# First layer: the scan's input coefficient formed beside the first norms, the keys' power and scaling taken earlier

## The chip, the cores and the metric

The kernel runs on one core of one Trainium2 chip. The metric is the device time of one execution in microseconds (us). Before the change three runs gave 987.22, 986.7 and 988.71 us, the median being 987.22 us.

## The reference

Two transformer blocks run one after the other on a sequence of 256 tokens and a width of 1024, in 32-bit floats. The first block has two layers. Each layer normalises, projects, and mixes the tokens in three ways: an S5 state space model on 256 channels, a gated spatial product on 256, and differential attention on 512. A convolution-gated MLP follows. The second block has dilated window, grouped and memory attention, with a gated merge. The change touches only the first layer of the first block, and there these two parts:

```python
# S5 mixer
lam = a_re + 1j * a_im
a_bar = exp(lam * dt)
b_bar = ((a_bar - 1.0) / lam)[..., None] * b_mat      # the input coefficient
bu = einsum("bsgh,gph->bsgp", u, b_bar)
states = associative_scan(a_bar, bu)
y = real(einsum("bsgp,ghp->bsgh", states, c_mat))

# differential attention
q = apply_rope(rms_norm(q, q_gain)); k = apply_rope(rms_norm(k, k_gain))
s = einsum(q, k) * scale                              # then a softmax by heads
```

The input coefficient is (a_bar - 1) / lam, one complex number for each group and state, held as 128 partitions by 16 columns. The kernel folds it into the output matrix c. The keys are scaled by the inverse root of their mean square, a power that GpSimd computes.

## The kernel before

**Weights.** Every product of activations with weights is made of three fp32r products: high part by high part, high by low, low by high. The weights stream through in 294 pairs of 128x1024. SyncE loads a pair into one of seven buffers `raw` (L432). ScalarE rounds it to its high part `whi` (L1100, six buffers). VectorE subtracts for the low part `wlo` (L1710, seven buffers). TensorE multiplies (L557 to L559 tile by tile for the queries, L594 to L596, L601 to L603) and counts the pairs it has used; ScalarE may overwrite a `whi` only once the pair six before is used. Pairs 0 to 3 are the queries, 4 to 7 the keys, 8 and 9 the channels of the state space model, 10 to 13 those of the spatial product, 14 to 17 the values.

**Order.** The order of the work is written out by hand, engine by engine. On VectorE `lo_upto(n)` stands wherever the low parts up to pair n are to be made, and the work of norms, attention and scan stands between these calls. `link` puts an instruction on a chain semaphore and, unless told otherwise, makes the next instruction wait for it.

**VectorE, first layer.** It prepares the state space parameters (L1744 to L1756), scales token tile 0 (L1719, `norm_scale`), and corrects its transposes (L1728, `norm_lo(0, 0)`). Then it takes the first amplitude power (L1764 to L1767), scales tile 1, prepares the phases (L1773 to L1778), and corrects tile 1 (`norm_lo(0, 1)`, again L1728). TensorE can multiply tile 1 only after that. The rotary tables follow (L1821), then for queries and keys a sum of squares by head (L1842), two products with the tables (L1830, L1831) and the rotation (L1835, L1836). Between queries and keys stands `coefficients()`, 15 linked instructions (L1788 to L1802). After the keys' rotation stand `phase_turns` (L353 to L355), pair 12, and the scaling of the keys (L1922). Then `rotate` turns the scan's inputs (L1847, L1848, L1853, L1854). It waits for the input products of TensorE and for the tables `etab`, which ScalarE makes from the turns (L364 to L369). After it come pair 14, the maxima of the first scores (L1864, L1867), `lambdas()`, pairs 15 and 16, and the two scans (L1939).

**GpSimd, first layer.** It powers the sums of squares (L1544 to L1546), builds the powers of the amplitude (L1569 to L1572), and expands the input matrix for its two parts c = 0 and 1 (`input_powers`: L411, L412, L414, L415). Then follow the queries' power (L1580, L1581), small work (L1596 to L1603), the fold of the coefficient into the output matrix (`folded`: L1551, L384 to L386), the keys' power (L1533, L1534), and the output powers, six instructions of 128x1024 (L396, L398, L400, twice). The fold waits for VectorE's coefficient, the keys' power for the keys' sum of squares.

**TensorE, first layer.** Query tile 0, transposes, query tile 1, key pairs 4 to 7 with transposes between, pairs 8 and 9, input products (L702), pairs 10 and 11, transposes of the keys (L757), pairs 12 and 13, first scores (L774), pairs 14 and 15, Toeplitz products (L676), pair 16, and so on. ScalarE rounds pair 16 (L1100) and then makes `etab`.

## Time and profile before

| | |
|---|---|
| median of three runs | 987.22 us |
| lowest, highest run | 986.7, 988.71 us |
| profiled execution, span | 986.2 us |
| TensorE busy | 954.6 us, 97% |
| VectorE busy | 695.7 us, 71% |
| ScalarE busy | 546.8 us, 55% |
| GpSimd busy | 258.5 us, 26% |

The profiled execution's own time is known here by its span, 986.2 us, alone; the lowest run lies 0.5 us above it and the median 1.0 us, which is what lies around the span. An engine's busy share says how much of the span it worked, not whether it set the end. For that the chain of waits is followed: it goes back from the last instruction, at each step to what released it. A timeline row gives start, duration, engine, line, operation, shapes, how many instructions are merged in it, and in brackets how long the engine sat idle before and what ended that.

### The profile page before, as it was taken

How to read it: one execution, taken by the hardware profiler on the slowest of the kernel's cores; microseconds unless marked ns; L12 is line 12 of the kernel's file. 1: busy time of each engine (PE TensorE's matmuls, PEld its weight loads, DVE VectorE, ACT ScalarE, POOL GpSimd, SP SyncE). 2: the span in 40 equal slices, each digit the busy share in tenths (PEclk: the TensorE clock that was granted, in tenths of full speed). 3: DMA queues.
4: the chain of work that ended last, by engine and by line, in shares of the span. 5: the costliest groups of instructions: out<-in, count | busy, mean ns of one | idle time of the engine just before them, and what ended most of it. 6: DMA issues, size and time to landing. Idle time of an engine off the chain costs nothing.

```text
span 986.2 us, 15775 instructions
## 1 busy us (share of the span) xinstructions
PE 954.6 (97%) x6139; PEld 838.7 (85%) x6143; DVE 695.7 (71%) x1074; ACT 546.8 (55%) x900; POOL 258.5 (26%) x196
## 2 busy tenths in 40 slices
PE   6979999999999999999999999999999999999997
PEld 4867789999978887799999988899787889888886
DVE  6998658778865688586777765558576755666785
ACT  7746556656743746756665554453454554555633
POOL 4890101676800021200455500003121300000030
PEclk9999999999999999999999999999999999999999
DMA  7622356665655542456665666575544445654452
GB/s 283 231 85 86 108 177 188 191 191 174 186 181 169 167 151 86 158 163 198 182 188 192 183 193 194 178 212 173 169 152 148 134 151 172 197 168 149 149 188 84
DMA packets 48473, 165.95 MB, mean 168 GB/s; under 512 B 6544, under 2 KB 7056, under 8 KB 48400
## 3 DMA queue, kind: packets, MB, share of 16 engines
q1 hardware_dynamic: 48400, 164.95, 53.2%
q8 instruction: 49, 0.80, 0.3%
q14 instruction: 24, 0.20, 0.1%
HBM read 162.83 MB, written 1.05 MB: 166 GB/s over the span
## 4 chain that ended last, share of the span: by engine, by line
PE 83%; DVE 9%; ACT 4%; issue 2%; POOL 1%; DMA 0%; DVEq 0%; POOLq 0%; SPq 0%; ACTq 0%
PE PJ L601 13%; PE PJ L603 13%; PE PJ L602 13%; PE PJ L596 10%; PE PJ L594 10%; PE PJ L595 10%; DVE wlo L1710 2%; PE PJ L557 2%; PE PJ L559 2%; PE PJ L558 2%; PE T L1041 1%; ACT whi L1100 1%; PE T L1032 1%; PE PJ L744 1%; PE S L648 1%
## 5 line engine op out<-in xcount | busy, mean ns | idle before, releaser
L1710 DVE TENSOR_TENSOR wlo<-raw,whi 128x1024 fp32r<-128x1024 f32 x294 | 370.3, 1290 | 95.8 <-ACT whi L1100 93.4
L1100 ACT ACTIVATE whi<-raw 128x1024 fp32r<-128x1024 f32 x294 | 303.0, 1062 | 77.1 <-DMA raw<-weights_in 70.5
L594 PE MATMUL PJ<-xthb,whi 128*128 128x256 f32 x864 | 242.9, 281 | 0.9 <-DVE wlo L1710 0.5
L596 PE MATMUL PJ<-xthb,wlo 128*128 128x256 f32 x864 | 242.3, 280 | 0.0
L595 PE MATMUL PJ<-xtlb,whi 128*128 128x256 f32 x864 | 241.4, 279 | 0.0
L601 PE MATMUL PJ<-whi,xthb 128*128 128x512 f32 (+1 forms) x432 | 173.9, 403 | 5.1 <-DVE wlo L1710 5.1
L603 PE MATMUL PJ<-whi,xtlb 128*128 128x512 f32 (+1 forms) x432 | 167.2, 387 | 0.0
L602 PE MATMUL PJ<-wlo,xthb 128*128 128x512 f32 (+1 forms) x432 | 167.0, 387 | 0.0
L594 PEld LDWEIGHTS PJ<-xthb,whi 128*128 128x128 f32 x864 | 163.0, 189 | 1.5 <-issue 1.3
L595 PEld LDWEIGHTS PJ<-xtlb,whi 128*128 128x128 f32 x864 | 163.0, 189 | 0.2
L596 PEld LDWEIGHTS PJ<-xthb,wlo 128*128 128x128 f32 x864 | 162.9, 189 | 0.0
L1632 POOL TENSOR_TENSOR gtd<-acc 128x512 f32<-128x512 f32 x22 | 96.4, 4380 | 149.2 <-ACT acc L1347 140.9
L2068 DVE SCALAR_TENSOR_TENSOR acc<-PJ,colv,acc 128x255 f32<-128x255 f32 (+1 forms) x176 | 72.5, 475 | 55.5 <-ACT acc L1342 54.8
L601 PEld LDWEIGHTS PJ<-whi,xthb 128*128 128x128 f32 x432 | 81.3, 188 | 25.6 <-issue 9.0
L1342 ACT ACTIVATE acc<-PJ,colv 128x256 f32<-128x256 f32 x88 | 42.5, 564 | 96.5 <-PE PJ L596 96.5
L603 PEld LDWEIGHTS PJ<-whi,xtlb 128*128 128x128 f32 x432 | 81.1, 188 | 17.2
L602 PEld LDWEIGHTS PJ<-wlo,xthb 128*128 128x128 f32 x432 | 81.4, 188 | 14.5
L601 PE MATMUL PJ<-whi,hth 128*128 128x512 f32 x144 | 56.1, 390 | 0.9 <-DVE wlo L1710 0.9
L603 PE MATMUL PJ<-whi,htl 128*128 128x512 f32 x144 | 56.0, 389 | 0.0
L602 PE MATMUL PJ<-wlo,hth 128*128 128x512 f32 x144 | 56.0, 389 | 0.0
L1689 POOL TENSOR_TENSOR merged<-merged,gt 128x512 f32<-128x512 f32 x6 | 9.6, 1625 | 160.7 <-DVE gt L2292 160.7
L601 PEld LDWEIGHTS PJ<-whi,hth 128*128 128x128 f32 x144 | 27.0, 188 | 6.8 <-issue 1.3
(399 smaller groups left out, 1341.1 us busy)
## 6 DMA issues: line engine op xcount, KB each, us to landing
raw<-weights_in SPq DMA_DIRECT2D x294, 512.0 KB, 3.6
rt<-bmerge_in SPq DMA_DIRECT2D x6, 256.0 KB, 4.2
xres<-x_in SPq DMA_DIRECT2D x2, 512.0 KB, 5.6
memx<-mem_in SPq DMA_DIRECT2D x2, 512.0 KB, 4.1
y_out<-xn SPq DMA_DIRECT2D x4, 256.0 KB, 2.3
rowv<-rows_in SPq DMA_DIRECT2D x1, 576.0 KB, 10.6
ptmp<-bexp_in SPq DMA_DIRECT2D x2, 256.0 KB, 6.6
cex<-cexp_in SPq DMA_DIRECT2D x2, 256.0 KB, 8.6
```

The lines of the kernel that those rows point to most:

```text
L557: pe.matmul(o, h, wh, start=(j == 0 and kk == 0), stop=False, skip_group_check=True)
L594: pe.matmul(o, a, xh[:, k, :], start=(first and f % 2 == 0), stop=False, skip_group_check=True)
L595: pe.matmul(o, a, xl[:, k, :], start=False, stop=False, skip_group_check=True)
L596: m = pe.matmul(o, b, xh[:, k, :], start=False, stop=last, skip_group_check=True)
L601: pe.matmul(o, h, wh, start=first, stop=False, skip_group_check=True)
L602: pe.matmul(o, h, wl, start=False, stop=False, skip_group_check=True)
L603: m = pe.matmul(o, lw, wh, start=False, stop=last, skip_group_check=True)
L1100: act.activation(whi[:, p % HIGHS, :], raw[:, p % LOADS, :], ACT.Copy).then_inc(hi_ready, 1)
L1342: act.activation(acc[:, j % 2, i, :], PJ[BUF[c]][:, i // 2, (i % 2) * TOK:(i % 2 + 1) * TOK], ACT.Identity, scale=colv[:, k + 2:k + 3], bi ...
L1632: pool.tensor_tensor(gtd[:, j % 2, :, :], acc[:, j % 2, 0:2, :], acc[:, j % 2, 2:4, :], ALU.mult).then_inc(sem("gated"), 1)
L1710: dve.tensor_tensor(wlo[:, p % LOADS, :], raw[:, p % LOADS, :], whi[:, p % HIGHS, :].bitcast(F32), ALU.subtract).then_inc(lo_ready, 1)
L2068: dve.scalar_tensor_tensor(out=acc[:, j % 2, i, sh:TOK], in0=PJ[BUF[c]][:, i // 2, (i % 2) * TOK:(i % 2 + 1) * TOK - sh], scalar=colv[:, k ...
```

## The change

Four things are moved, all in the first layer.

- The input coefficient is formed in other places and with 13 instructions instead of 15. Seven (new lines L1760 to L1766) stand before the scaling of tile 0, and give are/(are²+aim²) and aim/(are²+aim²). Six (L1788 to L1793), of 16 or 32 columns, stand after the phase preparation and before `norm_lo(0, 1)`. `coefficients()` is gone. In the fold rows 11 and 12 of the parameters change places.
- GpSimd takes the keys' power before the fold instead of after it.
- VectorE scales the keys before pair 12 and `phase_turns`, instead of after both.
- VectorE makes pairs 15 and 16 before `lambdas()` instead of after it.

```diff
@@ -376,7 +376,7 @@
         def fold_coefficient(eng, link, l, tmp):
 
             eng.wait_ge(sem("cex_landed"), 16 * (l + 1))
-            cr, ci, nci, ncr = (wide(sp_[:, r, 8 * l:8 * l + 8], 32, 2) for r in (9, 10, 11, 12))
+            cr, ci, nci, ncr = (wide(sp_[:, r, 8 * l:8 * l + 8], 32, 2) for r in (9, 10, 12, 11))
             re, im = cex[:, 0, :, :], cex[:, 1, :, :]
             t = tmp[:, 0:256].rearrange("p (s h) -> p s h", s=ST)
             for c, (i0, k0, i1, k1) in enumerate(((re, cr, im, nci), (re, nci, im, ncr))):
@@ -1601,8 +1601,8 @@
             link(pool.tensor_tensor(skip[:, 0:64], ident[:, 0:64], ident[:, 64:128], ALU.add))
             link(pool.tensor_tensor(skip[:, 0:32], skip[:, 0:32], skip[:, 32:64], ALU.add))
             link(pool.tensor_copy(ident4.rearrange("p (t h) -> p t h", t=STEP), wide(skip[:, 0:32], STEP)))
+            head_powers(0, 1)
             folded(0)
-            head_powers(0, 1)
             output_powers(pool, link, 0, 0, ptmp)
             output_powers(pool, link, 0, 1, ptmp)
             pool.sem_inc(sem("gpow_ready"), 1)
@@ -1756,6 +1756,14 @@
             link(dve.tensor_scalar(v[5], v[5], 3.1415925, -3.1415925, ALU.min, ALU.max))
 
             dve.sem_inc(sem("par_ready"), 1)
+            are, aim = col("are"), col("aim")
+            link(dve.tensor_tensor(v[16], are, are, ALU.mult), False)
+            link(dve.tensor_tensor(v[17], aim, aim, ALU.mult))
+            link(dve.tensor_tensor(v[16], v[16], v[17], ALU.add))
+            link(dve.reciprocal(v[13], v[16]))
+            link(dve.tensor_tensor(v[16], are, v[13], ALU.mult), False)
+            link(dve.tensor_tensor(v[15], aim, v[13], ALU.mult), False)
+            link(dve.tensor_tensor(v[17], aim, v[13], ALU.mult))
             norm_scale(0, xres, 0)
             lo_upto(1)
             norm_lo(0, 0)
@@ -1766,7 +1774,6 @@
             link(dve.tensor_tensor(apw[:, 0, 1, :], v[3], v[8], ALU.mult), False)
             link(dve.tensor_tensor(apw[:, 1, 1, :], v[3], v[6], ALU.mult))
             dve.sem_inc(sem("par_ready"), 1)
-            v[15] = apw[:, 1, 1, :]
             lo_upto(3)
             norm_scale(0, xres, 1)
             lo_upto(4)
@@ -1776,31 +1783,20 @@
             link(dve.tensor_tensor(v[19], v[19], v[18], ALU.subtract))
             link(dve.memset(chunks[:, :], 1.0))
             link(dve.tensor_tensor_scan(chunks[:, :], chunks[:, :], chunks[:, :], -1.0, ALU.mult, ALU.add))
+
+            from_one = apw[:, :, :, :].rearrange("p c t n -> p (c t) n")[:, 0:STEP + 3:STEP + 2, :]
+            link(dve.tensor_scalar(apw[:, 0, 0, :], apw[:, 0, 1, :], -1.0, None, ALU.add))
+            link(dve.tensor_tensor(sp_[:, 22:24, :], from_one, sp_[:, 16:18, :], ALU.mult), False)
+            link(dve.tensor_tensor(sp_[:, 13:15, :], from_one, sp_[:, 15:17, :], ALU.mult))
+            link(dve.tensor_tensor(v[9], v[22], v[23], ALU.add), False)
+            link(dve.tensor_tensor(v[10], v[14], v[13], ALU.subtract))
+            link(dve.tensor_scalar(sp_[:, 11:13, :], sp_[:, 9:11, :], -1.0, None, ALU.mult))
+            dve.sem_inc(sem("par_ready"), 1)
             norm_lo(0, 1)
             lo_upto(7)
             dve.wait_ge(sem("cst_landed"), 32)
             cosv = cs("cos").rearrange("p (t d) -> p t d", t=TT)
             sinv = cs("sin").rearrange("p (t d) -> p t d", t=TT)
-
-            def coefficients():
-
-                are, aim = col("are"), col("aim")
-                link(dve.tensor_scalar(v[14], apw[:, 0, 1, :], -1.0, None, ALU.add))
-                link(dve.tensor_tensor(v[16], are, are, ALU.mult))
-                link(dve.tensor_tensor(v[17], aim, aim, ALU.mult))
-                link(dve.tensor_tensor(v[16], v[16], v[17], ALU.add))
-                link(dve.reciprocal(v[16], v[16]))
-                link(dve.tensor_tensor(v[17], v[14], are, ALU.mult))
-                link(dve.tensor_tensor(v[18], v[15], aim, ALU.mult))
-                link(dve.tensor_tensor(v[17], v[17], v[18], ALU.add))
-                link(dve.tensor_tensor(v[9], v[17], v[16], ALU.mult))
-                link(dve.tensor_tensor(v[17], v[15], are, ALU.mult))
-                link(dve.tensor_tensor(v[18], v[14], aim, ALU.mult))
-                link(dve.tensor_tensor(v[17], v[17], v[18], ALU.subtract))
-                link(dve.tensor_tensor(v[10], v[17], v[16], ALU.mult))
-                link(dve.tensor_scalar(v[11], v[10], -1.0, None, ALU.mult))
-                link(dve.tensor_scalar(v[12], v[9], -1.0, None, ALU.mult))
-                dve.sem_inc(sem("par_ready"), 1)
 
             def lambdas():
 
@@ -1904,9 +1900,6 @@
                 head_sums(0)
                 lo_upto(s0 + 8)
                 rotary(0, A, "q_terms", "q_rot", s0 + (10 if l else 9))
-                if l == 0:
-                    lo_upto(s0 + 10)
-                    coefficients()
                 lo_upto(s0 + 11)
                 if l:
                     dve.wait_ge(sem("mixw_landed"), 32 * (l + 1))
@@ -1914,14 +1907,13 @@
                     lo_upto(s0 + 13)
                 head_sums(1)
                 rotary(1, B, "k_terms", "k_rot", s0 + (14 if l else 12))
-                if l == 0:
-                    phase_turns(dve, link, 0)
-                    lo_upto(s0 + 13)
                 dve.wait_ge(sem("hr_ready"), 2 * l + 2)
                 k8 = heads8(xn[:, :, 512:1024])
                 dve.tensor_tensor(k8, k8, wide(hr[:, 1, :].rearrange("p (t g) -> p t g", t=TT), QKD, 3), ALU.mult)\
                    .then_inc(sem("k_scaled"), 1)
                 if l == 0:
+                    lo_upto(s0 + 13)
+                    phase_turns(dve, link, 0)
                     dve.wait_ge(sem("mixw_landed"), 32)
                     dve.memset(wsts[64:128, :, 0:64], 0.0).then_inc(sem("wst_ready"), 1)
                 lo_upto(s0 + (17 if l else 14))
@@ -1967,8 +1959,8 @@
                 else:
                     lo_upto(s0 + 15)
                     batch_max(0)
+                    lo_upto(s0 + 17)
                     lambdas()
-                    lo_upto(s0 + 17)
                     scans()
                     lo_upto(s0 + 18)
                     gate_rows()
```

VectorE between tile 1's scaling and the rotary tables. Before:

```order
L1776 TENSOR_TENSOR sp_<-sp_ 128x16
L1777 MEMSET chunks 128x64
L1778 SCALAR_TENSOR_TENSOR chunks<-chunks 128x64
L1728 SCALAR_TENSOR_TENSOR xtlb<-T,colv,xthb 128x128 x8
L1710 TENSOR_TENSOR wlo<-raw,whi 128x1024 x3
```

Now:

```order
L1783 TENSOR_TENSOR sp_<-sp_ 128x16
L1784 MEMSET chunks 128x64
L1785 SCALAR_TENSOR_TENSOR chunks<-chunks 128x64
L1788 TENSOR_SCALAR apw<-apw 128x16
L1789 TENSOR_TENSOR sp_<-apw,sp_ 128x32
L1790 TENSOR_TENSOR sp_<-apw,sp_ 128x32
L1791 TENSOR_TENSOR sp_<-sp_ 128x16
L1792 TENSOR_TENSOR sp_<-sp_ 128x16
L1793 TENSOR_SCALAR sp_<-sp_ 128x32
L1728 SCALAR_TENSOR_TENSOR xtlb<-T,colv,xthb 128x128 x8
L1710 TENSOR_TENSOR wlo<-raw,whi 128x1024 x3
```

Six instructions now stand ahead of the eight corrections of tile 1, on which TensorE's second query tile waits.

VectorE from the keys' rotation to the scan's rotation. Before:

```order
L1836 TENSOR_TENSOR xn<-qh,sm 128x2x8x32
L353 TENSOR_TENSOR md<-sp_,chunks 128x512
L354 TENSOR_SCALAR md<-md 128x512
L355 SCALAR_TENSOR_TENSOR md<-md 128x512
L1710 TENSOR_TENSOR wlo<-raw,whi 128x1024
L1922 TENSOR_TENSOR xn<-xn,hr 128x2x512
L1926 MEMSET wsts 64x4x64
L1710 TENSOR_TENSOR wlo<-raw,whi 128x1024
L1847 TENSOR_TENSOR qh<-T,etab 128x1024
```

Now:

```order
L1832 TENSOR_TENSOR xn<-qh,sm 128x2x8x32
L1912 TENSOR_TENSOR xn<-xn,hr 128x2x512
L1710 TENSOR_TENSOR wlo<-raw,whi 128x1024
L353 TENSOR_TENSOR md<-sp_,chunks 128x512
L354 TENSOR_SCALAR md<-md 128x512
L355 SCALAR_TENSOR_TENSOR md<-md 128x512
L1918 MEMSET wsts 64x4x64
L1710 TENSOR_TENSOR wlo<-raw,whi 128x1024
L1843 TENSOR_TENSOR qh<-T,etab 128x1024
```

The scaling of the keys is now first of this group; the turns, from which ScalarE makes `etab`, have two instructions fewer between them and the rotation.

GpSimd, from the small work to the output powers, as a difference:

```order
 L1603 COPY cst<-cst 128x128
+L1533 TENSOR_SCALAR hr<-hsk 128x16
+L1534 TENSOR_TENSOR hr<-hr,mhalf 128x16
 L1551 TENSOR_SCALAR cst<-cst,colv 128x128 x2
 L384 TENSOR_TENSOR gpw<-cex,sp_ 128x8x32
@@ -46,6 +48,4 @@
 L385 TENSOR_TENSOR ptmp<-cex,sp_ 128x256
 L386 TENSOR_TENSOR gpw<-gpw,ptmp 128x8x32
-L1533 TENSOR_SCALAR hr<-hsk 128x16
-L1534 TENSOR_TENSOR hr<-hr,mhalf 128x16
 L396 TENSOR_TENSOR gpw<-gpw,apw 128x8x128
```

The keys' power has moved ahead of the eight instructions of the fold, which now wait behind it.

## Rows read from the trace of the kernel before

**Rows 1.** Page, part 1 (engine, busy us and share, instructions) and part 4 (chain that ended last).

```profile
PE 954.6 (97%) x6139; PEld 838.7 (85%) x6143; DVE 695.7 (71%) x1074; ACT 546.8 (55%) x900; POOL 258.5 (26%) x196
...
PE 83%; DVE 9%; ACT 4%; issue 2%; POOL 1%; DMA 0%; DVEq 0%; POOLq 0%; SPq 0%; ACTq 0%
```

**Rows 2.** Timeline of DVE, 7 to 23 us (start, duration, engine, line, operation, idle before).

```profile
7.76 0.88 DVE L1719 TENSOR_SCALAR xn<-xres,rstd 128x512 f32<-128x512 f32 x2 [2.76 <-POOL rstd L1546]
...
19.17 0.29 DVE L1778 TENSOR_TENSOR_SCAN chunks<-chunks 128x64 f32<-128x64 f32 x1
...
20.91 2.16 DVE L1728 SCALAR_TENSOR_TENSOR xtlb<-T,colv,xthb 128x128 fp32r<-128x128 f32 x8 [1.44 <-ACT xthb L1120]
```

**Rows 3.** Timeline of POOL, 19 to 27 us.

```profile
19.57 0.40 POOL L411 COPY vm<-bex 128x256 f32<-128x256 f32 x1
...
19.93 1.52 POOL L412 TENSOR_TENSOR vm<-bex,apw 128x768 f32<-128x768 f32 x1
...
21.41 1.53 POOL L414 TENSOR_TENSOR ptmp<-bex,apw 128x768 f32<-128x768 f32 x1
...
23.02 4.02 POOL L415 TENSOR_TENSOR vm<-vm,ptmp 128x768 f32<-128x768 f32 x1
```

**Rows 4.** Chain of waits, 28 to 34 us (start, duration, engine, tile, line), and POOL's timeline.

```profile
28.56 1.52 DVE ropeq L1821
...
28.35 1.57 POOL L412 TENSOR_TENSOR kmT<-bex,apw 128x768 f32<-128x768 f32 x1
...
31.53 1.86 POOL L415 TENSOR_TENSOR kmT<-kmT,ptmp 128x768 f32<-128x768 f32 x1
```

**Rows 5.** Stretches: PE busy, PEld, DVE, ACT, POOL (x instructions), PEclk, DMA.

```profile
21.57:45.58 24.01, 24.01 (x137) 21.03 (x138) 22.65 (x36) 18.27 (x26) 20.34 (x17) 1.00 0.64 215
```

**Rows 6.** Timeline of DVE, 42 to 46 us.

```profile
42.03 0.29 DVE L1788 TENSOR_SCALAR sp_<-apw 128x16 f32<-128x16 f32 x1
...
45.31 0.17 DVE L1802 TENSOR_SCALAR sp_<-sp_ 128x16 f32<-128x16 f32 x1
```

**Rows 7.** Timeline of ACT, 55 to 59 us.

```profile
55.02 1.06 ACT L1100 ACTIVATE whi<-raw 128x1024 fp32r<-128x1024 f32 x1 [5.78 <-PE PJ L603]
...
57.81 0.63 ACT L369 ACTIVATE etab<-md 128x512 f32<-128x512 f32 x1
```

**Rows 8.** Timeline of DVE, 54 to 73 us.

```profile
56.06 3.00 DVE L1922 TENSOR_TENSOR xn<-xn,hr 128x1024 f32<-128x1024 f32 x1
...
61.90 1.21 DVE L1847 TENSOR_TENSOR qh<-T,etab 128x1024 f32<-128x1024 f32 x1
...
64.28 0.69 DVE L1853 TENSOR_TENSOR sw<-qh 128x512 f32<-128x512 f32 x1
...
64.89 2.46 DVE L1854 TENSOR_TENSOR sw<-qh 128x512 f32<-128x512 f32 x1
...
67.27 2.98 DVE L1710 TENSOR_TENSOR wlo<-raw,whi 128x1024 fp32r<-128x1024 f32 x1
...
71.61 0.92 DVE L1867 SCALAR_TENSOR_TENSOR st_<-st_,hr 128x8 f32<-128x8 f32 x1
```

**Rows 9.** Timeline of POOL, 64 to 73 us.

```profile
64.34 2.46 POOL L396 TENSOR_TENSOR gpw<-gpw,apw 128x1024 f32<-128x1024 f32 x1
...
69.25 3.25 POOL L400 TENSOR_TENSOR gpw<-gpw,ptmp 128x1024 f32<-128x1024 f32 x1
```

**Rows 10.** Timeline of PE, 59 to 76 us.

```profile
59.12 1.09 PE L757 MATMUL S<-cst,xn 128*128 128x128 f32 x8 [1.49 <-DVE xn L1922]
...
70.39 0.47 PE L601 MATMUL PJ<-whi,xthb 128*128 128x512 f32 x1 [3.15 <-DVE wlo L1710]
```

**Rows 11.** Stretch at 400 us, columns as in Rows 5, then PE's timeline.

```profile
400.00:402.00 2.00, 1.93 (x5) 1.60 (x6) 0.00 (x0) 1.67 (x5) 0.00 (x0) 0.50 0.90 367
...
400.07 3.57 PE L744 MATMUL PJ<-md,wglus 128*128 128x256 f32 x8 [0.94 <-issue]
...
101.18 1.97 PE L744 MATMUL PJ<-md,wglus 128*128 128x256 f32 x8 [0.94 <-issue]
```

## The prediction

> **What bounds the kernel now.** I read the page first, then the chain of waits, then the timelines of the engines over the first 105 us. TensorE is busy for 97% of the span and makes up 83% of the chain; VectorE has 9% [rows 1]. Behind the first layer's attention TensorE hardly waits, so a change here pays only if it lets TensorE begin that run sooner. Before it, through most of the first layer, the chain runs through VectorE. TensorE waits there 1.49 us for the scaled keys and 3.15 us for the low part of pair 14 [rows 10].
>
> Two stretches matter. In the first, TensorE works from 21.57 to 45.58 us with no gap: 24.01 busy of 24.01 us [rows 5]. It begins when VectorE has corrected the first transposes of tile 1, which VectorE starts at 20.91 us after 1.44 us idle [rows 2]. In the second, VectorE rotates the scan's inputs at 61.90 us [rows 8]. ScalarE had the tables for it at 57.81 + 0.63 = 58.44 us. These tables stand behind ScalarE's rounding of pair 16, which began at 55.02 us, the moment TensorE had used pair 10 [rows 7].
>
> **The part that is removed.** `coefficients()` runs from 42.03 to 45.31 + 0.17 = 45.48 us [rows 6]. With the issue of the next pair that is 3.6 us on VectorE's path. The next pairs' high parts are there by then, so VectorE really moves up. But it can't use all of it. The tables of ScalarE hang on TensorE's pair 10 and not on VectorE, so the rotation can't start before 58.44 us. The cap is 61.90 - 58.44 = 3.46 us.
>
> **The seven early instructions.** VectorE sits idle for 2.76 us before it scales tile 0 [rows 2]. Small linked instructions follow each other every 0.21 us (15 took 3.45 us, with their waits [rows 6]), so seven take at most 1.5 us. They are done before GpSimd delivers the first norm. Cost: nothing. If that cover were gone, they would cost those 1.5 us on the first transposes.
>
> **The six later instructions.** They start when the scan of the chunks ends, at 19.17 + 0.29 = 19.46 us. Alone they would take six times 0.21 us or less, 1.25 us, and end by 20.7 us, before 20.91 us. But GpSimd expands the input matrix at that time: L411 from 19.57, L412 from 19.93, L414 from 21.41, L415 from 23.02 us [rows 3]. What that does to a small VectorE instruction with two operands in SBUF is seen later. The rotary table of 128x128 that starts at 28.56 us takes 1.52 us and ends at 30.08; GpSimd's L412 runs from 28.35 to 29.92 us [rows 4]. L1867, 128x8, takes 0.92 us and ends at 72.53 us, when L400 ends at 72.50 [rows 8, 9]. So a VectorE instruction, however small, waits until a GpSimd instruction under way is over, and gets in before the next. The six are four links: L1788; L1789 with L1790; L1791 with L1792; L1793. The first gets through before L411 reads. The second meets L411, and L1790 or the third meets L412, to 19.93 + 1.52 = 21.45 us. The link behind that meets L414, to 21.41 + 1.53 = 22.94 us. The rest, two issues, gets in before L415 reads. The corrections then start at about 23.2 us in place of 20.91, and **TensorE's tile 1 is 2.3 us late**. Bounds: nothing if no instruction is held; if the last one is also held by L415, which takes 1.86 us where it is free [rows 4], the start is 23.10 + 1.86 = 24.96 us and the loss 4.05. I take 2.3 since two of the three holds follow whatever the order at the first one.
>
> The Trainium skill (SBUF — State Buffer, Who interferes with whom) says that VectorE with two SBUF inputs and GpSimd exclude each other for a whole instruction, and that the one issued first keeps the port. By that, rows 4, 8 and 9 agree, and the six instructions are held; without it they would be free and the change would give the whole 3.46 us.
>
> **The sum.** TensorE carries these 2.3 us without loss to pair 10, since it has no gap to absorb them [rows 5]. So ScalarE's tables come at 58.44 + 2.3 = 60.74 us, and the rotation starts at 60.74 in place of 61.90: 1.16 us sooner. VectorE waits there for them, with nothing left of its own lead.
>
> **Keys.** L1922 ended at 59.06 us, held by GpSimd for 1.8 of its 3.00 us (L1847, of as many columns, takes 1.21) [rows 8]. Now the power no longer stands behind the fold, and the scaling not behind the turns and a pair; VectorE reaches it 3.6 us (coefficients) and some 3 us (turns and a pair) before 56.06 us, so near 49.5 us, and near 52 us with TensorE's delay. TensorE's wait of 1.49 us before L757 goes [rows 10], and 2.3 come in, so its first scores end 0.8 us later, near 68.1 us. The wait for pair 14 up to 70.39 us covers this [rows 10]. What is late next is pair 14 itself, on VectorE. GpSimd's fold, moved behind the power, costs it an idle start but the products that read its output powers stand behind pairs 14 and 15 on TensorE, of 12 matmuls each, at least 5 us after 70.39 us, and the powers ended at 72.50 [rows 9, 10].
>
> **Lambdas.** Pairs 15 and 16 come some 1.4 us sooner, but VectorE's next scan does not, since the same instructions stand before it, and from there the chain goes on through VectorE. Cost and gain: nothing on the path; TensorE's wait before pair 15 only moves to a later place. If VectorE were no longer on the path, this part would be worth up to 1.4 us.
>
> **The phase of the holds.** From the rotation on VectorE's L1853, L1854 and pair 14 alternate with GpSimd's output powers. Before, the second and third were held: 2.46 and 2.98 us, against 0.69 for L1853 [rows 8]. With both engines shifted, there may be one hold more or one less, 1.8 us each way. TensorE's first scores set the other end: 70.25 (end of pair 14) - 68.1 = 2.2 us gain at most. So this case gives a gain between -0.7 and 2.2, and I take 1.2.
>
> 987.22 - 1.2 = **986.0 us**, own range 985.0 to 987.9. In the profiled execution the span of 986.2 would become 985.0; the median of the runs lies 1.0 us above the span.
>
> **Rivals.**
> 1. *The six instructions slip through.* They are 16 or 32 columns wide, and the trace shows no such instruction at the back-to-back boundary of L411 and L412. Against it stands L1867, as narrow and held [rows 8, 9]. Then all 3.46 us come: 983.8 us, with the phase of the holds 982.0 to 985.6.
> 2. *Slower: one hold more, and TensorE's clock.* L1793 is held by L415. Tile 1 starts 4.05 us late, TensorE is idle for over 4 us, and the rotation starts 4.05 - 3.46 = 0.6 us later than before: 987.8 us. The point from which it decides is 3.46 us of delay. If in addition the granted clock falls to 0.50, which is 1.2 of 2.4 GHz, as it did at 400 us after two pauses (L744 took 3.57 us there, 1.97 in the first layer [rows 11]), TensorE loses 1.6 us more, before pair 10: 3.46 - 4.05 - 1.6 = -2.2, so 989.4 us. For it: the pause is longer than any behind which the clock stayed up (3.15 us [rows 10]).
> 3. *The holds eat it.* GpSimd's fold starts after the keys' power and later than before relative to VectorE, so the output powers meet VectorE at one more place: 1.2 - 1.8, and 987.2 us once L1867's own hold of 0.75 us (0.92 less the 0.17 of so narrow an instruction as L1802) is free. The change does then what it says, and nothing comes of it.
>
> The Trainium skill (TensorE: Matmul & The Clock Gate, What's actually happening) says that an idle TensorE is put back to half its clock. Here 400 us agrees, and the pause before 70.39 us does not. By the page rival 2 would deserve more than I give it.
>
> **How the numbers follow.** Forecast 0.45; rival 1 0.25; rival 2 0.15 (0.07 at 987.8, 0.08 at 989.4); rival 3 0.15. A measurement of this kernel tells about 0.2% from no change, 2.0 us, so faster means below 985.2 and slower above 989.2. Faster: nearly all of rival 1 (0.23) and the far edge of the forecast (0.07), 0.30. Slower: 0.08 of rival 2 and a little for a clock fall at another place, where every pause now lies at another time (1.6 us each), 0.10. The rest, 0.60, is the same. The range reaches from 983.6, the likeliest of rival 1, to 988.6, and leaves out the fall of the clock and the far edge of rival 1.
>
> **What would show it.** In the new profile: six small instructions at 19.5 us that end near 20.7 (rival 1), 23.2 (forecast) or 25 us (rival 2), one or two of them 1.4 us long; the start of tile 1 on TensorE at 21.6, 23.9 or 25.6 us; the rotation's start at ScalarE's tables and no longer behind a pair; no TensorE wait before L757; how often L1853, L1854 and pair 14 are over 1.3 us long; the granted clock at 20 to 30 us and at 400 us. I would be wrong in the step itself if the rotation still started behind VectorE's own work, or if TensorE had caught up its delay before pair 10.

## The result, and the profile after

The change makes the kernel slower. Six runs have a median of 991.43 us (990.97 to 993.49), and six of the kernel before, taken with them, 987.41 us (986.7 to 988.71): a ratio of 1.0034, 95% interval 1.0024 to 1.0044. The forecast was 986.0 us with 983.6 to 988.6 as its range, and 0.10 for slower. (The ratio, here and in the table below, is the estimate on record and not the quotient of the two medians, which is 1.0041 here: the loss is 3.4 us by the one and 4.0 by the other.) The profiled execution is the slowest of the six, 993.49 us, with a span of 991.7 us, 5.5 more than before, so its rows show more of the loss than the median has.

The page, part 1 and the chain's shares, which answer to [rows 1]. VectorE has less of the chain (9% before, 7% now), but TensorE has more of it (83% before, 86% now):

```profile
PE 959.7 (97%) x6139; PEld 842.9 (85%) x6143; DVE 689.4 (70%) x1072; ACT 547.2 (55%) x900; POOL 262.5 (26%) x196
...
PE 86%; DVE 7%; ACT 4%; issue 2%; POOL 1%; DMA 0%; DVEq 0%; POOLq 0%; SPq 0%; ACTq 0%
```

**First place, 19 to 34 us.** The timeline of VectorE (start, duration, line, idle before), then of TensorE:

```profile
19.66 0.17 DVE L1788 TENSOR_SCALAR apw<-apw 128x16 f32<-128x16 f32 x1
19.86 0.31 DVE L1789 TENSOR_TENSOR sp_<-apw,sp_ 128x32 f32<-128x32 f32 x1
20.10 0.18 DVE L1790 TENSOR_TENSOR sp_<-apw,sp_ 128x32 f32<-128x32 f32 x1
20.31 1.38 DVE L1791 TENSOR_TENSOR sp_<-sp_ 128x16 f32<-128x16 f32 x1
21.62 0.16 DVE L1792 TENSOR_TENSOR sp_<-sp_ 128x16 f32<-128x16 f32 x1
21.81 1.39 DVE L1793 TENSOR_SCALAR sp_<-sp_ 128x32 f32<-128x32 f32 x1
23.35 2.16 DVE L1728 SCALAR_TENSOR_TENSOR xtlb<-T,colv,xthb 128x128 fp32r<-128x128 f32 x8
...
24.01 0.79 PE L557 MATMUL PJ<-whi,xthb 128*128 128x512 f32 x1 [3.08 <-DVE xtlb L1728]
```

Two of the six instructions last 1.38 and 1.39 us instead of 0.17, each until one of GpSimd's is over (at 21.66 and 23.16 us):

```profile
20.09 1.57 POOL L412 TENSOR_TENSOR vm<-bex,apw 128x768 f32<-128x768 f32 x1
21.62 1.54 POOL L414 TENSOR_TENSOR ptmp<-bex,apw 128x768 f32<-128x768 f32 x1
```

The corrections start at 23.35 us (20.91 before [rows 2]), TensorE at 24.01 (21.57 before [rows 5]). Then comes what the forecast's sum had not counted. Stretches of TensorE (bounds, length, busy us of PE, PEld, DVE, ACT, POOL with their instructions, then PEclk, DMA share, GB/s):

```profile
22.00:26.00 4.00, 1.99 (x5) 1.60 (x6) 3.85 (x10) 2.42 (x5) 3.76 (x4) 0.64 0.01 2
26.00:30.00 4.00, 4.00 (x11) 3.13 (x10) 4.00 (x3) 1.06 (x1) 4.00 (x2) 0.50 0.34 126
30.00:34.00 4.00, 4.00 (x19) 3.28 (x19) 3.93 (x4) 1.94 (x2) 3.25 (x2) 1.00 0.83 270
```

The granted clock fell to 0.50, which is 1.2 of 2.4 GHz, in the pause of 3.08 us, and was up again by 30 us: 11 matmuls in 4 us at the one level, 19 at the other. The 24 matmuls of tile 1 took 8.5 us instead of 5.7.

**Second place, 60 to 80 us.** ScalarE's rounding of pair 16 and the last of its tables, then VectorE:

```profile
60.25 1.06 ACT L1100 ACTIVATE whi<-raw 128x1024 fp32r<-128x1024 f32 x1 [5.80 <-PE PJ L603]
...
63.05 0.63 ACT L369 ACTIVATE etab<-md 128x512 f32<-128x512 f32 x1
```

```profile
63.88 1.23 DVE L1843 TENSOR_TENSOR qh<-T,etab 128x1024 f32<-128x1024 f32 x1 [4.07 <-ACT etab L369]
...
66.27 2.43 DVE L1849 TENSOR_TENSOR sw<-qh 128x512 f32<-128x512 f32 x1
68.62 2.45 DVE L1850 TENSOR_TENSOR sw<-qh 128x512 f32<-128x512 f32 x1
70.99 2.98 DVE L1710 TENSOR_TENSOR wlo<-raw,whi 128x1024 fp32r<-128x1024 f32 x1
...
75.33 0.89 DVE L1863 SCALAR_TENSOR_TENSOR st_<-st_,hr 128x8 f32<-128x8 f32 x1
...
79.78 2.48 DVE L1931 TENSOR_TENSOR_SCAN sw<-decay,sw 128x512 f32<-128x512 f32 x2
```

Pair 16 is rounded 5.23 us later than before [rows 7]: 2.4 by the held instructions, and 2.8 on the way from there, which e2 below puts down to the clock. The rotation starts at the tables, as forecast, 1.98 us later than before instead of 1.16 sooner. Then L1849 is held too (2.43 us, 0.69 before [rows 8]), which makes 3.69 us at the scans, 79.78 where the trace before has 76.09:

```profile
76.09 2.48 DVE L1939 TENSOR_TENSOR_SCAN sw<-decay,sw 128x512 f32<-128x512 f32 x2
```

GpSimd's timeline tells why there is one hold more:

```profile
52.03 4.02 POOL L1551 TENSOR_SCALAR cst<-cst,colv 128x128 f32<-128x128 f32 x2
...
61.76 1.99 POOL L396 TENSOR_TENSOR gpw<-gpw,apw 128x1024 f32<-128x1024 f32 x1
...
72.96 3.23 POOL L400 TENSOR_TENSOR gpw<-gpw,ptmp 128x1024 f32<-128x1024 f32 x1
```

Its six output powers run from 61.76 to 76.19 us, from 55.25 to 72.50 before. The fold in front of them starts at 52.03 us, in VectorE's run of two-input instructions, and its first two take 4.02 us; they took 1.35 us before.

**Third place, 104 us.** TensorE's gate products, which answer to [rows 11]:

```profile
104.87 3.58 PE L744 MATMUL PJ<-md,wglus 128*128 128x256 f32 x8 [0.94 <-issue]
```

They took 1.97 us before behind the same pause of 0.94 us; now the clock is at 0.51 from 105 to 108 us. From here on the distance is 5.4 us (405.50 against 400.07 us for the same products of the second layer) and 5.5 at the end.

Between the second and the third place this trace has one more fall, which the kernel before does not have in its own: 0.59 from 74 to 76 us and 0.56 from 76 to 78, behind a pause of 3.36 us ahead of pair 14.

```profile
74.11 0.57 PE L601 MATMUL PJ<-whi,xthb 128*128 128x512 f32 x1 [3.36 <-DVE wlo L1710]
```

It cost the path nothing that the rows show: the distance is 3.69 us at the scans and still 3.69 at the start of the gate's products (104.87 against 101.18).

### The profile page after: what moved, and what is told of

It reads as the page before. It is cut to its first block, busy times and chain, and to the rows that moved or that the text cites. A ratio compares the mean times of both kernels' runs of the same rounds, so it can differ in the third digit from the quotient of the medians.

```text
span 991.7 us, 15774 instructions
## 1 busy us (share of the span) xinstructions
PE 959.7 (97%) x6139; PEld 842.9 (85%) x6143; DVE 689.4 (70%) x1072; ACT 547.2 (55%) x900; POOL 262.5 (26%) x196
## 4 chain that ended last, share of the span: by engine, by line
PE 86%; DVE 7%; ACT 4%; issue 2%; POOL 1%; DMA 0%; DVEq 0%; POOLq 0%; SPq 0%; ACTq 0%
PE PJ L601 14%; PE PJ L603 13%; PE PJ L602 13%; PE PJ L596 10%; PE PJ L594 10%; PE PJ L595 10%; PE PJ L557 2%; PE PJ L558 2%; PE PJ L559 2%; DVE wlo L1710 2%; PE T L1041 1%; ACT whi L1100 1%; PE T L702 1%; PE PJ L744 1%; PE T L1032 1%
## 5 line engine op out<-in xcount | busy, mean ns | idle before, releaser
L1710 DVE TENSOR_TENSOR wlo<-raw,whi 128x1024 fp32r<-128x1024 f32 x294 | 365.9, 1276 | 95.4 <-ACT whi L1100 93.4
```

Of the source, the lines that this page charges most:

```text
L1710: dve.tensor_tensor(wlo[:, p % LOADS, :], raw[:, p % LOADS, :], whi[:, p % HIGHS, :].bitcast(F32), ALU.subtract).then_inc(lo_ready, 1)
```

## The experiments

Two theories went in. **H**: the held coefficient instructions, and the clock behind them. **O**: GpSimd's output powers, put behind a later fold, hold VectorE around the scan's rotation. All times are medians over the 4 (e5) to 12 executions of five rounds; the kernel before was run beside each group and lay between 987.68 and 988.30 us. Only one execution of each kernel has a trace. The last three columns are from that one: start of the rotation, end of the last output power, start of the scans (us).

```
kernel                         time    ratio [95%]             rot    powers  scans
before                         -       -                       61.90  72.50   76.09
change                         991.43  1.0034 [1.0024,1.0044]  63.88  76.19   79.78
e1  GpSimd waits               990.47  1.0020 [1.0011,1.0028]  62.71  73.33   76.92
e2  TensorE kept busy          989.84  1.0015 [1.0005,1.0025]  61.47  73.82   77.41
e3  six at the old place       989.87  1.0012 [1.0002,1.0022]  58.33  75.24   76.49
e4  coefficient alone          990.33  1.0013 [1.0003,1.0022]  65.70  71.80   78.59
e5  e1, fold first             997.10  1.0099 [1.0084,1.0114]  72.48  71.48   84.64
e6  e3, fold first             995.67  1.0078 [1.0066,1.0091]  70.54  69.53   82.09
e7  keys alone                 991.86  1.0042 [1.0030,1.0054]  60.01  75.31   78.36
e8  e5, lambdas first          994.68  1.0077 [1.0064,1.0089]  72.11  71.10   83.69
e9  e3, diagonals first        988.07  0.9996 [0.9987,1.0006]  59.96  72.38   75.97
e10 e1, diagonals first        987.80  1.0003 [0.9993,1.0013]  59.67  72.43   76.03
e11 e3, three powers out       985.51  0.9973 [0.9961,0.9984]  58.50  66.20   72.38
e12 before, three powers out   985.93  0.9972 [0.9963,0.9982]  61.85  64.20   72.42
e13 e9, two fillers            992.25  1.0045 [1.0028,1.0061]  59.89  72.35   75.95
e14 before, two fillers        991.56  1.0037 [1.0023,1.0050]  61.78  72.38   75.98
e15 e2, two fillers            993.61  1.0057 [1.0041,1.0072]  60.97  73.32   76.91
e16 e9, filler at pair 14      989.49  1.0015 [1.0005,1.0025]  59.71  72.17   75.75
e17 before, filler at pair 14  987.87  0.9999 [0.9990,1.0009]  62.03  72.63   76.23
e18 e2, filler at pair 14      990.66  1.0029 [1.0018,1.0041]  64.05  72.34   78.52
```

### The change undone in parts: e1 to e4

**e1** lets GpSimd expand the input matrix only when the coefficient is there:

```diff
             pool.wait_ge(sem("bex_ready"), 1)
+            pool.wait_ge(sem("par_ready"), 4)
             input_powers(pool, link, 0, 0, x_tile(0), ptmp)
```

> The change, but GpSimd begins to expand the input matrix only when VectorE has finished the six later coefficient instructions. Theory H (holds, then clock): the six instructions lost 2.4 us to GpSimd's L412 and L414, the pause of TensorE that came of it let the granted clock fall, and both together made pair 10 5.2 us late. Here nothing holds them: the corrections of tile 1 start near 21.0 us instead of 23.35, TensorE has no pause over 1 us there and no clock of 0.50 before 70 us, the scan's rotation starts near 58.7 us, and the time is 983.0 to 985.5 us, below before. Rival O (order): what lost the time is the new order of power, fold and scaling, whose output powers meet VectorE at another place; then the time stays near the change's, 989 to 992 us, though the corrections come early.

The six now run free, 0.17 to 0.19 us each. VectorE's timeline:

```profile
20.35 0.18 DVE L1794 TENSOR_SCALAR sp_<-sp_ 128x32 f32<-128x32 f32 x1
20.77 2.16 DVE L1729 SCALAR_TENSOR_TENSOR xtlb<-T,colv,xthb 128x128 fp32r<-128x128 f32 x8 [0.24 <-ACT xthb L1120]
```

Yet the kernel is no faster than before, and H by itself falls. The test is not a clean one, though (e3 is): in its trace TensorE's clock fell at another place, with no pause but the 0.71 us ahead of L702 (0.70 in the kernel before, behind which the clock stayed up): the stretch 54 to 56 us has PE busy for 2.00 of 2.00 us at 0.50, where the kernel before has 1.00.

```profile
54.00:56.00 2.00, 2.00 (x6) 1.61 (x6) 1.82 (x4) 0.00 (x0) 1.84 (x3) 0.50 0.00 0
```

**e2** leaves the holds and keeps TensorE busy in the pause ahead of tile 1 (26 transposes of the identity into the bank that is written next):

```diff
+                if l == 0:
+                    keep_busy(B[:, 1, :], 26)
                 tile_pairs(f"q{l}", 1, 0, range(4), xth, xtl, ready=32 * l)
```

> The change, with 26 transposes of the identity into a free bank between TensorE's tile 0 and tile 1 of the queries, so that it is not idle while the corrections are late. Theory H: the corrections still start near 23.35 us and tile 1 near 24.0 us, but the granted clock stays at 1.00, the 24 matmuls of tile 1 take 5.5 us instead of 8.5, pair 10 is 2.4 us late instead of 5.2, and the time is 2.5 to 3.5 us under the change's: 987.5 to 989. Rival O: no difference to the change beyond 1 us, since the order stays.

L1728 starts at 23.72 us, as late as in the change, but the clock stays up. From the corrections to the rounding of pair 16 it takes 34.1 us instead of 36.9:

```profile
24.00:26.00 2.00, 2.00 (x13) 1.71 (x12) 2.00 (x9) 1.25 (x4) 1.83 (x3) 1.00 0.02 4
```

So the fall behind the 3.08 us pause cost 2.8 us on this path. Scans at 77.41 us, 1.32 later than before; the time is above what H gave and still above before. By the ratios the fillers take away 1.9 of the change's 3.4 us and leave 1.5.

**e3** puts the six back between the queries' and the keys' rotation (after pair 10), where the old 15 stood:

```diff
                 rotary(0, A, "q_terms", "q_rot", s0 + (10 if l else 9))
+                if l == 0:
+                    lo_upto(s0 + 10)
+                    coefficients()
```

> The change, with the seven early instructions where the change has them, but the six later ones put back at the old place of the coefficients, between queries and keys. Theory H: they cost 1.1 us on VectorE there in place of 3.6, the corrections start near 20.9 us, the clock stays up, the rotation starts at ScalarE's tables near 58.6 us, and the time is 983.0 to 985.5 us. Rival O: 989 to 992 us.

Here the whole lead is there: the rotation starts at 58.33 us, 3.57 sooner than before. And the scans start 0.40 us *later*. VectorE's timeline shows where it went, two pairs and a 128x4 instruction:

```profile
68.90 4.13 DVE L1710 TENSOR_TENSOR wlo<-raw,whi 128x1024 fp32r<-128x1024 f32 x2
72.95 2.31 DVE L1806 TENSOR_SCALAR hb<-colv 128x4 f32<-128x4 f32 x1
```

They took 2.36 and 0.16 us in the kernel before. L1806 ends when GpSimd's last power does:

```profile
72.03 3.21 POOL L400 TENSOR_TENSOR gpw<-gpw,ptmp 128x1024 f32<-128x1024 f32 x1
```

**e4** makes only the coefficient's change (order of GpSimd, keys and lambdas as in the kernel before).

> The kernel before with the coefficient's change alone: GpSimd's power after the fold, the keys scaled after the turns, lambdas first. Theory H: slower than before by about as much as the whole change, 989.5 to 992.5 us, with the corrections at 23.3 us and a clock of 0.50 behind it. Rival O: faster than before by up to 3 us, 984.5 to 987.

The time lies inside H's range, but at 1.3 us by its ratio the loss is less than half of the whole change's 3.4, and H had said about as much. The six are held as in the change (corrections at 23.18 us), the clock is at 0.51 from 24 to 26 us, and it falls again at 54.7. The tables come at 65.50 us, so the last output power, though it ends at 71.80 us and 0.70 sooner than before, meets the rotation's last product (L1850, 2.86 us), and the scans start 6.79 us behind it where it was 3.59.

### The order of the fold and the keys: e5 to e8

**e5** is e1, and **e6** is e3, with GpSimd's fold ahead of the keys' power again:

```diff
-            head_powers(0, 1)
             folded(0)
+            head_powers(0, 1)
```

> The change, with GpSimd waiting for the coefficient before it expands the input matrix (as in e1), and with the fold taken before the keys' power again, as in the kernel before. Theory of two causes (H: the held coefficient instructions and the fall of TensorE's clock behind them; O: the fold behind the keys' power makes GpSimd's output powers late, and these hold VectorE around the scan's rotation): with both away the lead of VectorE comes through as far as ScalarE's tables let it. Corrections of tile 1 at 20.8 us, tables near 58.5, rotation near 58.7, output powers from 51 to 54 us on, the maxima's last instruction at 69 to 71 us (72.53 before), the scans at 73 to 74.5 (76.09). Time 983.5 to 986 us against some 987.5 of the kernel before. H alone: already reached in e1, so no better than e1, 990. O alone: the same as the two causes. Rival (clock): TensorE's granted clock falls somewhere else once its pauses lie elsewhere, 1.6 us for each 3.4 us at 0.50, and takes the lead back: maxima and scans early as above, but 986.5 to 989 us.

> The change with the six later coefficient instructions at the coefficient's old place (as in e3), and the fold before the keys' power again. Seven instructions stay early, so VectorE is some 2.4 us ahead of the kernel before there. Theory of two causes: corrections of tile 1 at 19.7 to 20.9 us, rotation near 58.3 us, output powers from 52 to 55 us, and no such holds of pairs 14 to 16 as in e3 (4.13 us for two, and 2.31 for the lambdas' first instruction); scans at 73 to 75 us where e3 had 76.49; 983.5 to 986.5 us. If e3's scans were late for another reason (the order of pairs 15, 16 and the lambdas), they stay at 76 to 77 us and the time at 987 to 990.

They lie 11.1 and 9.2 us above the upper ends of their forecasts, the worst misses of the study. VectorE in e5:

```profile
56.16 2.94 DVE L1913 TENSOR_TENSOR xn<-xn,hr 128x1024 f32<-128x1024 f32 x1 [4.71 <-POOL hr L1534]
59.02 2.98 DVE L1711 TENSOR_TENSOR wlo<-raw,whi 128x1024 fp32r<-128x1024 f32 x1
61.93 2.88 DVE L353 TENSOR_TENSOR md<-sp_,chunks 128x512 f32<-128x512 f32 x1
64.84 2.07 DVE L354 TENSOR_SCALAR md<-md 128x512 f32<-128x512 f32 x1
66.94 2.33 DVE L355 SCALAR_TENSOR_TENSOR md<-md 128x512 f32<-128x512 f32 x1
```

VectorE waits 4.71 us for the power, behind which GpSimd begins the output powers at once. So the scaling, pair 12 and the three turns come each behind one of them, the turns take 7.3 us together (0.69 + 0.43 + 0.69 us in the kernel before), and the tables come at 71.77 us. O as stated (early powers are good) falls; what is left of it is that the *number of VectorE's instructions that meet a power* counts. With the keys scaled ahead of the turns, the power has to stand ahead of the fold; the reverse, the power moved alone, was not run.

**e7** makes these two parts alone in the kernel before:

> The kernel before with the keys' part alone: GpSimd takes the keys' power ahead of the fold, VectorE scales the keys ahead of pair 12 and the turns. The coefficient stays as it was, the lambdas too. Theory O: output powers start 2 to 4 us later than the 55.25 us of before, meet the rotation and pair 14, and the maxima's last instruction and the scans come 0.5 to 2 us later (scans 76.6 to 78): 987.5 to 990 us. H alone: this order does nothing (TensorE's wait for the scaled keys goes, pair 14 sets the end): scans at 76.1, 986.5 to 988 us. My prediction's reading of the part, a gain by the phase turns having fewer instructions behind them, would give 985.5 to 987.

It is at least as slow as the whole change (ratio 1.0042 against 1.0034). The rotation starts 1.89 us sooner, the scans 2.27 us later. Output powers from 60.93 to 75.31 us hold the second product of the rotation, pair 14 and two of the lambdas' sums, of which one row:

```profile
73.00 2.39 DVE L1813 CUSTOM_DVE_ANT_0 sqs<-ug 128x64 f32<-128x64 f32 x1
...
78.36 2.48 DVE L1938 TENSOR_TENSOR_SCAN sw<-decay,sw 128x512 f32<-128x512 f32 x2
```

TensorE then pauses 4.13 us ahead of pair 14 and 3.07 ahead of pair 15, and its clock falls in both:

```profile
69.27 0.76 PE L601 MATMUL PJ<-whi,xthb 128*128 128x512 f32 x1 [4.13 <-DVE wlo L1710]
...
77.45 0.77 PE L601 MATMUL PJ<-whi,xthb 128*128 128x512 f32 x1 [3.07 <-DVE wlo L1710]
```

**e8** is e5 with `lambdas()` ahead of pairs 15 and 16 again.

> As the first kernel of this call, and the lambdas before pairs 15 and 16 again, as in the kernel before. It tells what the move of the lambdas is worth when the lead is there. Prediction's reading: up to 1.4 us if VectorE isn't on the path and nothing if it is, so the same as the first kernel within 0.5 us, or up to 1.4 us slower. Rival: the lambdas behind two pairs meet GpSimd's last output power (in e3 their first instruction took 2.31 us), so with them first this kernel is 0.5 to 2 us faster than the first: scans below 73 us.

Its median is 2.4 us lower, on five executions against four and with intervals that overlap. The lambdas don't show in it: from the end of the maxima to the scans it is 3.56 us in e5 and 3.57 in e8, since the powers are over by then. The scans of e8 start 0.95 us sooner in its trace, all of it from ahead of that stretch; what makes up the rest was not found.

### The shared stretch: e9 to e12

A third theory: from the keys' rotation to the scans, GpSimd's fold and powers and VectorE's instructions take turns, and a lead of VectorE only meets more of them. **e9** (on e3) and **e10** (on e1) take GpSimd's first two instructions of the fold, which need no coefficient, into its idle time ahead of the keys' power:

```diff
+            skip_diagonals(0)
             head_powers(0, 1)
             folded(0)
```

> As e3 (coefficient's six at the old place, power before the fold), but GpSimd takes the two scalings of the skip diagonal (first lines of the fold, which need no coefficient) before the keys' power, where it sat idle for 3.00 us in e3. Theory of the shared stretch: from the keys' rotation to the scans the end is set by GpSimd's work that must lie there, fold and output powers, and every lead of VectorE is eaten by holds until the last output power ends (75.24 us in e3). The two scalings took 4.02 us there, so the output powers start some 3 to 4 us sooner, near 55 to 56 us instead of 58.92, end near 71 to 72.5, and the scans come at 73 to 75 us instead of 76.49. Time: 1.5 to 3.5 us less than e3, so 986.5 to 988.5 against 988 of before in the last measurement. Rival: GpSimd is starved by VectorE's run of two-input instructions (48 to 59 us) whatever it executes, and the powers still start at 58 us or later: time as e3. Clock rival: scans as forecast, but falls of the granted clock add 1.6 us each.

> As e1 (GpSimd waits for the coefficient before the input matrix) with the two scalings before the keys' power. There GpSimd was idle for only 0.83 us before the power, so the scaling delays the power by about 0.5 us, which VectorE hardly meets (keys scaled at 50.3 to 51 us). Shared stretch theory: output powers start near 55 to 56 us instead of 58.73, end near 70 to 71 instead of 73.33, scans at 74 to 75.5 instead of 76.92. If the clock stays up at 52 us, tables at 59 instead of 62.5 us and another 1 us. Time 986 to 989 us (e1: 990.47).

The last power ends 2.86 us sooner in e9 than in e3, and 0.90 in e10 than in e1. Times fall by 1.8 and 2.7 us, to that of the kernel before, and no lower: the scans stand at 75.97 and 76.03 us, with the rotation 1.9 and 2.2 us earlier than before. The scans moved by only 0.5 and 0.9 us, so part of what the times gained came from elsewhere. In e9 all of L1858, L1859, pair 14 and L1872 are held:

```profile
62.34 2.56 DVE L1858 TENSOR_TENSOR sw<-qh 128x512 f32<-128x512 f32 x1
64.81 2.44 DVE L1859 TENSOR_TENSOR sw<-qh 128x512 f32<-128x512 f32 x1
67.18 2.97 DVE L1716 TENSOR_TENSOR wlo<-raw,whi 128x1024 fp32r<-128x1024 f32 x1
```

**e11** (on e3) and **e12** (on the kernel before) put one fill with zeros in the place of the last three output powers, the imaginary half of them:

```diff
             output_powers(pool, link, 0, 0, ptmp)
-            output_powers(pool, link, 0, 1, ptmp)
+            link(pool.memset(gpw[:, 1, :, 1:STEP + 1, :], 0.0))
```

> e3 with the last three of the six output powers left out and one fill of the same tile with zeros in their place. Left out: the imaginary half of the output powers in the first layer. Shared stretch theory: the lead now gets through: the last output power ends near 65 to 66 us, pairs 15 and 16 take 1.2 us each, the lambdas' first instruction 0.2 us, scans at 72 to 73.5 us (76.49 in e3); time 984 to 986.5 us. If the powers are not what holds the scans, they stay at 75.5 us or later and the time near 989.

> The kernel before with the same three output powers left out. Shared stretch theory: the holds behind 64.3 us go (second product of the rotation 1.8, pair 14 1.8, maxima's last instruction 0.75 us; TensorE's first scores allow some 2.2 to 3 of it): scans at 73 to 74 us, 985 to 987 us. So it gains as the kernel with the lead does, and what is between the two, 0.5 to 1.5 us of the 3.5 us of lead, is what the lead is worth when the powers are out of the way. If VectorE's own length set the end, the two would differ by the whole 3.5 us.

Both kernels lie below before, by 2.8 and 2.4 us by their medians (2.7 and 2.8 by the ratios), and the scans of both at 72.4 us: first e11, then e12.

```profile
72.38 2.48 DVE L1937 TENSOR_TENSOR_SCAN sw<-decay,sw 128x512 f32<-128x512 f32 x2
```

```profile
72.42 2.47 DVE L1939 TENSOR_TENSOR_SCAN sw<-decay,sw 128x512 f32<-128x512 f32 x2
```

With three powers fewer the scans start 4.11 us sooner than in e3 and 3.67 sooner than before: the powers hold them back in both kernels. And a rotation that starts 3.35 us sooner (58.50 against 61.85) is again worth 0.04 us. But that the two agree is in part chance, since the maxima ahead of the scans (67.20 and 67.23 us) are released by different things. In e11 pair 14 is held by a power, which ends at 66.20 us because the fold started late; in e12 the powers are over at 64.20, nothing holds pair 14, and VectorE waits for TensorE's first scores. Pair 14 and GpSimd's power in e11, then the maxima in e12:

```profile
63.92 3.37 DVE L1710 TENSOR_TENSOR wlo<-raw,whi 128x1024 fp32r<-128x1024 f32 x1
63.52 2.68 POOL L400 TENSOR_TENSOR gpw<-gpw,ptmp 128x1024 f32<-128x1024 f32 x1
```

```profile
67.23 1.42 DVE L1864 TENSOR_REDUCE st_<-S 128x4 f32<-128x512 f32 x2 [0.56 <-PE S L774]
```

In e11 those scores are there at 65.37 us, 1.8 sooner than in e12 (67.18). So the lead is not worthless by itself: it was lost to the powers that are left.

The two last columns of the table now read as one sum: the scans start when the last power has ended and VectorE has done what it then has left. In every trace but e12's the last power holds an instruction of VectorE. In the kernel before, the change, e1, e2, e9, e10 and e13 to e17 it is the maxima's last one, and the scans come 3.58 to 3.60 us behind the power. In e3 and e7 it is one of the lambdas, and they come 1.25 and 3.05 us behind. In e11 and e18 it is pair 14, in e4 the rotation's last product and in e5, e6 and e8 pair 13, and they come 6.2 to 13.2 us behind. So in e3 the lead was worth 2.34 us (3.59 less 1.25), and the power that ends 2.74 us later than before takes that back and 0.40 more.

### The clock: e13 to e18

`keep_busy` transposes the identity. **e13, e14, e15** (on e9, before, e2) do it ahead of pair 14 and ahead of the gate's products:

```diff
                 if l == 0:
+                    emptied("v0")
+                    keep_busy(PJ[buf("v0")][:, 0, :], 22)
                     project("v0", pairs=[0, 1])
...
+                    if l == 0:
+                        pe.wait_ge(sem("da_exp"), 16)
+                        keep_busy(S1, 8)
                     pe.wait_ge(sem("g_ready"), 2 * (l + 1))
```

> As e9 (scans at 75.97 us, as before; median 988.07), and TensorE transposes the identity 22 times while it waits for pair 14 and 8 times before the gate's products near 100 us. Clock theory: e9's falls at 69.9 and 100.7 us go, 1.6 us each, with scans unchanged at 76.0 us: 984.5 to 986.5 us, and below the kernel before in this call. Rival: the falls only move to another pause, or the fillers lie in TensorE's way (0.12 us each): 987 to 989 us.

> The kernel before with the same fillers. Its profile shows no fall at 70 or 100 us, but its runs range over 4 us, so some of them have falls somewhere. Clock theory: 985.5 to 987.5, up to 1.5 us below before in this call, with fewer runs above 988. Rival (fillers cost or do nothing): within 0.5 us of before or slower.

> The change with 26 fillers ahead of tile 1 (as e2) and the two groups of the last two kernels. Clock theory: no falls at 23, 70 to 75 and 103 to 105 us, scans at 77.4 us as in e2, 1.3 us later than before: 986.5 to 988.5 us, so 1.3 us above the second kernel of this call, and what is left of the loss is the holds. Rival: the loss is not the clock's: 989.5 to 991.5 us, as e2 or more.

These measured their own mistake. The eight fillers wait for the last exponentials, which end at 102.0 us, so TensorE pauses for 1.97 us where it had 0.94, starts the gate's products 2.65 us later, and the clock is at 0.50 from 102 to 106 us. In e14:

```profile
102.10 1.94 PE L628 MATMUL S<-cst 128*128 128x128 f32 x8 [1.97 <-ACT sm L1247]
103.83 3.62 PE L747 MATMUL PJ<-md,wglus 128*128 128x256 f32 x8
```

**e16, e17, e18** are the same without the eight.

> e9 with the 22 fillers ahead of pair 14 only. Clock theory: the fall at 70 us goes, the one at 100 us may stay or go; scans at 76.0, TensorE's gate products at 101.1 us: 985.5 to 987.5 us, at least 1 us below before in this call if both falls go. Rival: the fall only comes elsewhere: 987.5 to 988.5 us, as e9.

> The kernel before with the 22 fillers ahead of pair 14 only. It had no fall there, so: the same as before within 0.5 us (987.5 to 988.5), scans 76.1, gate products 101.1 us. If a pause filled here lets the clock stay up at the later pauses as well, up to 1.5 us less.

> The change with 26 fillers ahead of tile 1 and 22 ahead of pair 14. Holds alone: scans 0.8 to 1.3 us later than before (76.9 to 77.4), so 0.8 to 1.3 us above the second kernel of this call, 988.5 to 989.5. If the clock still falls once more than there (at 103 us), another 1.6 us: 990 to 991. If the median of e2 (989.84) isn't undercut, the fall at 74 us was not part of the loss.

e17 is the kernel before. e16 is 1.4 us slower than e9 although the fall at 70 us is gone from its profile and the scans are as early; nothing in its profile explains that. Its executions have a mean granted clock of 0.9936 against e9's 0.9950, so falls at other places are one reading, but no trace shows them, and it stays open. e18 is 0.8 us above e2 and 0.8 below the change: its profile has the fall of the kind seen in e1 and e4, at 53 us, and by its own expectation a median that doesn't undercut e2's says that the fall at 74 us was not part of the loss. So a filler takes a fall away from one pause, and what the clock does at the next place isn't in hand.

How much of the loss is the clock? The mean granted clock over the span was 0.9927 in the six of the change and 0.9945 to 0.9959 in those of the kernel before (11 to 35 in each group). The difference, 0.0018 to 0.0032, of 988 us would be 1.8 to 3.2 us of TensorE's time at full clock. That is an estimate from above: not every fall lies on the path (the one at 74 us in the change), and the time follows the mean only loosely. Executions of the kernel before at 0.994 took 986.44 to 990.48 us in one group, and e17, at 0.9966 against 0.9951, was no faster. What is measured is e2: with the fillers against the first fall the ratio is 1.0015 (1.0005 to 1.0025) instead of 1.0034 (1.0024 to 1.0044). So about half of the loss is likely that one fall, and the 1.5 us that are left fit the 1.32 us at the scans. e2's trace has the fall at the gate's products too; what that one adds to the medians isn't shown, since most executions of the kernel before have a lower clock than its traced one (0.997).

No version that computes everything is faster than the kernel before. e9, e10 and e17 equal it. That it would pay to take the output powers out of this stretch, by moving the Toeplitz products behind other pairs on TensorE, is suggested by e12 (2.4 to 2.8 us) but wasn't tried.

## Why the prediction was wrong

**Right.** *The six later instructions*: corrections forecast at about 23.2 us, measured 23.35, by two holds (L1791, L1793), with L411 passed freely. *The seven early instructions*: nothing on the path to speak of; tile 0 is scaled at 7.92 us for 7.76, and its idle time fell from 2.76 to 1.60 us. *The part that is removed*: the rotation starts at ScalarE's tables, 0.2 us behind them, and where nothing delays tile 1 it comes as much sooner as the cap said (e3: 3.57 us, cap 3.46). *Lambdas*: worth nothing, 3.56 us from maxima to scans before and after. TensorE's wait before the keys' transposes (L757) is gone.

**Wrong, the sum's first term.** "TensorE carries these 2.3 us without loss to pair 10": it carried 2.4 us of delay and 2.8 of clock, so the tables came at 63.68 us in place of 60.74. I had given the fall 0.08 and a price of 1.6 us, and bound it to a pause of over 4 us, because the clock had stayed up behind 3.15 us [rows 10]. Behind 3.08 us it fell, and in e1 with none but 0.71 us before it. One pause without a fall is no bound.

**Wrong, the keys.** "GpSimd's fold, moved behind the power, costs it an idle start but the products that read its output powers stand behind pairs 14 and 15": costed at nothing. I looked for readers of the powers and not for what the powers meet on the way. e7, this part alone, is 4.2 us above the kernel before, as much as the whole change. Of that, 2.27 us stand at the scans in its trace; the clock falls ahead of pairs 14 and 15 and at the gate's products besides. The losses of the parts don't add up (e4, the coefficient's part alone, loses 1.3 us), and none of the runs splits e7's any further.

**Wrong, the phase of the holds.** "There may be one hold more or one less", and I took 1.2 us of gain. It was one hold more, 1.74 us on L1849. The deeper error is that the gain was read from the tables and not from GpSimd's queue: with the whole lead there, in e3, the scans start 0.40 us later than before, because the last output power ends 2.74 us later (75.24) and the work left behind it is only 2.34 us shorter. Rival 3 named this mechanism, with 0.15, and gave 987.2 us for it (its own terms give 987.1); rival 2 named the fall of the clock. I had kept the two as alternatives, and both came. Their sum would still have been only 988.8 us; the first fall alone cost 2.8 us of the way to pair 16 in the trace, where I had 1.6 for one.

The Trainium skill (SBUF — State Buffer, Who interferes with whom) lets a VectorE instruction with two SBUF inputs and a GpSimd instruction that reads SBUF exclude each other. The trace agrees: the rotation's first products, one input in PSUM, take 1.21 to 1.23 us in every kernel, also where they run beside GpSimd's powers, and in the change the next three, with both inputs in SBUF, take 2.43 to 2.98 us.

## What to carry to other kernels

Where two engines exclude each other, read a stretch as one queue: add up what both must do in it, and ask where the last instruction that can hold something ends, and what the other engine then has left to do. A lead of that other engine counts only in the second term and can be lost in the first, as the 3.57 us of e3 were. Leaving out half of the suspected work, with and without the lead, shows whether that work is what holds; whether the lead is worth anything then is read from what released the next stage in each of the two, and not from the two times being equal. Where two rivals' mechanisms can hold together, give their sum a chance too; and count a pause of TensorE that comes near the longest one seen as a risk of a slower clock, priced by the matmuls behind it.

## What the runs showed of the hardware that I had not expected

- The clock fell from 52 to 58 us in e1 with PE busy for all of it, in the input products (L702) and then in pair 10; in the kernel before the same work ran at 1.00. Executions of one kernel differ too: 29 of the kernel before had mean clocks of 0.993 to 0.997 and spans of 984.6 to 989.1 us.
- GpSimd is held as well. In VectorE's run of two-input instructions GpSimd's two scalings of 128x128 took 4.02 us in place of 1.35, while VectorE's of 128x1024 took their free 1.22 us; moved ahead of the power (e9), the two took 2.08.
- A TENSOR_SCALAR of one input, 128x512, is held as well: L354 took 0.43 us in the kernel before, 0.72 in the change and 2.07 in e5.
